# A two-layer hybrid backbone on one core: eight split places, moved modulation, and layer 1's modulation slots as TensorE products

## The chip, the cores and the metric

The kernel runs on one core of a Trainium2 chip. The metric is the device time of one execution in microseconds (us). The profiled execution gives times from its span's start; its granted TensorE clock has two levels, 1.0 (2.4 GHz) and 0.5 (1.2 GHz).

## The reference, cut to what matters

512 latent and 256 context tokens of width 1024 pass through two layers. `w_mod` gives six vectors per layer and per stream, which scale, shift and gate the tokens:

```python
for l in range(DEPTH):
    mod_x = silu(c) @ w_mod[l] + b_mod[l]        # 6 x 1024, latent
    mod_c = silu(c_ctx) @ w_mod[l] + b_mod[l]    # 6 x 1024, context
    mix = token_mixers((h * (1 + ca) + sa) @ w_in[l])     # attention A, B, D and an HGRN2 scan C
    h = layer_norm(ALPHA * h + ga * (mix @ w_out[l]))
    f = conv_ffn(h * (1 + cf) + sf)              # up 1024 -> 2 x 2816, conv of 3, silu(a) * v, down
    h = layer_norm(ALPHA * h + gf * f)
```

The context is dropped after layer 0's last use of it.

## The kernel before, in words

All engines run one hand-ordered program with semaphores. Tokens lie on partitions in `H` (six tiles of 128); a stage first turns them with TensorE transposes (`turn_latent`, `turn_context`), modulates them on the way out of PSUM, and multiplies by weights.

**Weights and ring.** The weights come as 148 slots of 1 MB in the order `STREAM`, loaded by SyncE's queue one after another into a ring of three places, `WR`. `ring_plan` gives each slot a place; a load waits until the slot that held its place is released. SyncE issues in order, so a load also waits for all loads ahead of it. In the FFN only places 1 and 2 are used. A `mod` slot holds 256 columns of `w_mod` (24 slots per layer), an `up` slot the two halves (a and v) of one of 22 FFN column tiles, j = 0 to 21.

**Modulation.** Layer 0's 24 slots are done by TensorE: `mod_products` (8 products in four groups of 32 columns of the array, 16 records), ScalarE copies the rows (`copy_mod`), `mod_columns` adds and turns them (2 products), VectorE adds the bias (`mod_out`). Layer 1's 24 slots lie in layer 0's FFN: VectorE multiplies and adds the slot's eight tiles for both streams (`mod_macs`, 16 operations, releasing the place with `mac_done`), then TensorE sums over partitions (`mod_sums`, 4 products with one column).

**FFN up.** Products are made of two fp32r parts: ScalarE copies the high part of an up half (`high_part`), GpSimd subtracts to the low part (`low_part`, which releases the place with `w_low`), and TensorE does 48 products per half with context (24 of 512 columns, 24 of 256). `first_units` does j = 0, interleaved with the turning of the tokens; `ffn_up` the rest. The high part of half n+2 is made right after half n's sum was read. Two halves are in the split buffer `WS`.

**Out and down projections.** `k_tiles` are 16 (out) or 44 (down) steps. For each, ScalarE writes high parts of the activations and the weight rows into one of `entries` (6 places for out), VectorE (`low_parts`) and GpSimd make the low parts. A place is free when its step is used, or, for the last four steps of each half of the columns, when all tiles of that half are summed (`acc_sum`). VectorE does the first 12 `low_parts` before it takes any sum; then `fold_norm` (three small operations), then per tile: gate, add, statistics; `normalise` follows one tile behind, after GpSimd's power (`rstd_ready`). With context there are 12 sums for 8 PSUM banks, so sum 8 waits until VectorE has read sum 0 (`acc_read`).

**Start.** SyncE loads constants (1.6 MB), x (2.1 MB, issued at 2.1 us), the context (1.05 MB), then slots (1.05 MB each). TensorE waits for both, turns latent (ScalarE copies) and context (VectorE copies), does eight modulation slots, and then the first projection.

Of the kernel before, what the change touches and what calls it, by code (L numbers as in the profile page):

```python
# [7 lines left out]
P = 128  # L8
# [63 lines left out]

def uses():

    u = [("mod", 0, i, 0) for i in range(MOD_FIRST)]
    for l in range(DEPTH):
# [37 lines left out]
def hybrid_backbone(nc, weights, x, ctx_in, consts, masks, params, bias_d, ln_rows, out):  # L114
# [14 lines left out]
    with stack:  # L129
# [20 lines left out]
        EU = nc.alloc_sbuf_tensor_at("EU", [P, 8 * ENTRY], f32r, offset=starts["U"])  # L150
# [3 lines left out]
        def bank(n, cols=512):  # L154
# [6 lines left out]
        entries = ([EU[:, a:a + ENTRY] for a in [e * ENTRY for e in range(5)] + [FT * TOK]],  # L161
                   [t[:, e * ENTRY:(e + 1) * ENTRY] for t in (XH, XL, EW) for e in range(2)])
# [50 lines left out]
        maccs = [W[:, a:a + 1024].rearrange("p (r v c) -> p r v c", r=2, v=2) for a in (5120, 6144)]  # L213
        macc_of = lambda mac: maccs[1][:, mac % 2]
# [63 lines left out]
        xc_raw = sem("xc_raw")  # L278
# [71 lines left out]
        mac_done = sem("mac_done")  # L350
# [234 lines left out]
        def split_parts(q, nt):  # L585

            e = q.entry
            return (e[:, 0:nt * P], e[:, TOK:TOK + nt * P]), (e[:, 2 * TOK:2 * TOK + 512], e[:, 2 * TOK + 512:])
# [34 lines left out]
        def lat_bank(m, k):  # L623
            return bank((4 if m % 2 else 6) + k % 2)

        def ctx_bank(m, k):
            return bank((0, 6, 4)[m] + k % 2, 256)
# [16 lines left out]
        def _(sp):  # L644
# [16 lines left out]
        def _(pe):  # L661
# [20 lines left out]
            def mod_sums(mac, out4):  # L682

                pe.wait_ge(mac_done, mac - (24 - MOD_FIRST))
                for jj in range(2):
                    for v in range(2):
                        mm = pe.matmul(out4[:, 2 * jj + v:2 * jj + v + 1], macc_of(mac)[:, v, jj * P:(jj + 1) * P], ones,
                                       start=True, stop=True)
# [5 lines left out]
            def turn_latent(m, k):  # L694
                freed, count = ((x_raw, 0), (x_val, 0), (x_lat, KT), (x_val, KT))[m]
                if k >= 2:
                    pe.wait_ge(freed, count + k - 1)
                for t in range(NLT):
# [5 lines left out]
            def turn_context(m, k):  # L704
                freed, count = ((xc_raw, 0), (xc_val, 0), (x_ctx, KT))[m]
# [28 lines left out]
            def projections(l, js):  # L734
                for j in js:
# [24 lines left out]
                    mm.then_inc(job_sum, 1)  # L760
                    for n in j.mods:
# [17 lines left out]
            def hgrn(l):  # L779
# [6 lines left out]
                def score_maps(u):  # L786
                    par = u.g % 2
                    pe.wait_ge(qe, u.no + 1)
                    pe.wait_ge(zeroed, l + 2)
# [215 lines left out]
            def ffn_up(l):  # L1005
                us = ups_of[l]
                for u in us[2:]:
                    if u.freed:
                        wait_all(pe, (conv_done, u.freed[0]), (mod_done, u.freed[1]))
                    if u.kind == "mod":  # L1010
                        mod_sums(u.mac, PS[u.pos])
# [9 lines left out]
                    mm.then_inc(up_sum, 1)  # L1021

# [16 lines left out]
        def _(act):  # L1039
# [19 lines left out]
            for k in range(KT):  # L1059
# [5 lines left out]
            def modulate(m):  # L1065
                l, j0, with_ctx = stages[m]
                if m == 0:
                    act.wait_ge(mod_done, MOD_FIRST)
                    act.wait_ge(xc_raw, KT)
                    for k in range(KT):  # L1070
                        c = x3[:, k, SEQ:TOK]
                        act.activation(c, c, ACT.Identity, bias=mod3[:, l, j0 + k, 1:2],
                                       scale=mod3[:, l, j0 + 8 + k, 1:2]).then_inc(x_ctx, 1)
# [131 lines left out]
            def gates(m):  # L1205
# [822 lines left out]
```

## Time and profile before

| | |
|---|---|
| times of three runs | 2188.62, 2193.34, 2197.52 us; median 2193.34 us |
| profiled execution | 2196.59 us, span 2194.1 us, mean granted clock 0.953 |
| busy, share of the span | TensorE 93%, VectorE 60%, GpSimd 39%, ScalarE 34% |
| layer 0's FFN up, j = 1 to 21, at 711.7 to 1108.3 us | 396.6 us |
| layer 0's and layer 1's out projections, from 597.4 and 1740.5 us | 81.0 and 52.2 us |

How to read it: TensorE is busy nearly everywhere, so a change is worth what it takes from or adds to TensorE's own time and its waits. A place where TensorE idles names the engine that ended the wait.

### The profile page before, as it was taken

How to read it: one execution, taken by the hardware profiler on the slowest of the kernel's cores; microseconds unless marked ns; L12 is line 12 of the kernel's file. 1: busy time of each engine (PE TensorE's matmuls, PEld its weight loads, DVE VectorE, ACT ScalarE, POOL GpSimd, SP SyncE). 2: the span in 40 equal slices, each digit the busy share in tenths (PEclk: the TensorE clock that was granted, in tenths of full speed). 3: DMA queues.
4: the chain of work that ended last, by engine and by line, in shares of the span. 5: the costliest groups of instructions: out<-in, count | busy, mean ns of one | idle time of the engine just before them, and what ended most of it. 6: DMA issues, size and time to landing. Idle time of an engine off the chain costs nothing.

```text
span 2194.1 us, 30749 instructions
## 1 busy us (share of the span) xinstructions
PE 2032.8 (93%) x11900; PEld 1640.3 (75%) x11900; DVE 1312.8 (60%) x2695; ACT 744.5 (34%) x1428; POOL 857.2 (39%) x636
## 2 busy tenths in 40 slices
PE   6998999989988799999989999899799978999997
PEld 3665877867767688888878877577787767788786
DVE  2028878776566999889952441775867662222444
ACT  2113343246631222222243321342336623333442
POOL 0005545220134365333443333453511246655643
PEclk8999998999998899999999999998799989999999
DMA  7541010010010323333331111111010112222321
GB/s 299 192 173 39 20 39 20 28 65 1 21 58 20 119 112 134 105 128 115 118 110 54 65 58 58 39 39 39 20 73 2 40 58 77 88 100 99 115 89 68
DMA packets 24127, 169.82 MB, mean 77 GB/s; under 512 B 2608, under 2 KB 2608, under 8 KB 4784
## 3 DMA queue, kind: packets, MB, share of 16 engines
q1 hardware_dynamic: 22544, 157.90, 20.1%
q10 hardware_dynamic: 1440, 9.96, 1.1%
q8 instruction: 96, 1.57, 0.3%
q14 instruction: 47, 0.39, 0.1%
HBM read 165.76 MB, written 2.10 MB: 77 GB/s over the span
## 4 chain that ended last, share of the span: by engine, by line
PE 71%; DVE 14%; issue 6%; POOL 4%; DMA 2%; ACT 2%; SPq 0%; DVEq 0%; ACTq 0%; POOLq 0%
PE PS L1018 20%; PE PS L943 17%; PE PS L758 10%; PE PS L752 7%; DVE W L1334 3%; PE PS L879 3%; PE PS L904 3%; PE PS L863 2%; DMA WR<-in_weights 2%; PE PS L794 2%; PE PS L869 1%; PE PS L999 1%; DVE W L1332 1%; PE PS L671 1%; POOL WS L1901 1%
## 5 line engine op out<-in xcount | busy, mean ns | idle before, releaser
L1018 PE MATMUL PS<-XH,WS 128*128 128x512 f32 x2016 | 545.2, 357 | 8.0 <-POOL WS L1901 7.4
L1018 PEld LDWEIGHTS PS<-XH,WS 128*128 128x128 f32 x2016 | 361.0, 190 | 64.1 <-issue 4.9
L1018 PE MATMUL PS<-XL,WS 128*128 128x512 f32 x1008 | 358.9, 356 | 0.0
L1901 POOL TENSOR_TENSOR WS<-WR,WS 128x1024 fp32r<-128x1024 f32 x88 | 213.1, 2424 | 314.3 <-ACT WS L1203 314.2
L758 PE MATMUL PS<-WR,X 128*128 128x256 f32 x1248 | 292.1, 395 | 5.6 <-DMA WR<-in_weights 5.6
L758 PEld LDWEIGHTS PS<-WR,X 128*128 128x128 f32 x1248 | 246.7, 200 | 43.9 <-DMA WR<-in_weights 6.6
L1258 ACT ACTIVATE W<-PS,PR 128x768 f32<-128x768 f32 (+1 forms) x88 | 77.9, 885 | 450.5 <-PE PS L1018 388.2
L752 PE MATMUL PS<-X,WR 128*128 128x512 f32 (+1 forms) x576 | 210.9, 524 | 10.1 <-issue 6.8
L1018 PEld LDWEIGHTS PS<-XL,WS 128*128 128x128 f32 x1008 | 191.9, 190 | 26.8
L1788 DVE SCALAR_TENSOR_TENSOR W<-PS,PR,W 128x511 f32<-128x511 f32 (+1 forms) x132 | 83.0, 657 | 202.2 <-ACT W L1258 202.1
L1334 DVE SCALAR_TENSOR_TENSOR W<-WR,SC,W 128x256 f32<-128x256 f32 x336 | 199.1, 634 | 6.0
L752 PEld LDWEIGHTS PS<-X,WR 128*128 128x128 f32 x576 | 114.3, 203 | 92.7 <-issue 80.9
L1851 POOL TENSOR_SCALAR W<-U 128x128 f32<-128x128 f32 x48 | 40.5, 844 | 325.2 <-DVE U L1495 201.3
L1890 POOL TENSOR_TENSOR EU<-WR,EU 128x512 fp32r<-128x512 f32 x32 | 52.9, 1681 | 237.6 <-ACT EU L1234 237.5
L943 PE MATMUL PS<-EU 128*128 128x512 f32 x480 | 117.2, 406 | 18.6 <-DVE W L1752 7.9
L943 PE MATMUL PS<-XH 128*128 128x512 f32 x480 | 116.4, 398 | 9.9 <-POOL XH L1890 9.9
L943 PEld LDWEIGHTS PS<-EU 128*128 128x128 f32 x480 | 93.5, 196 | 41.4 <-DVE W L1752 10.5
L943 PEld LDWEIGHTS PS<-XH 128*128 128x128 f32 x480 | 92.3, 193 | 29.9 <-issue 10.4
L1150 ACT ACTIVATE W<-W 128x64 f32<-128x64 f32 (+1 forms) x120 | 35.2, 356 | 203.2 <-DVE W L1524 203.2
L1870 POOL TENSOR_TENSOR W<-W 128x1024 f32<-128x1024 f32 (+1 forms) x48 | 100.0, 2084 | 9.2 <-PE PS L801 9.2
L1593 DVE COPY_PREDICATED W<-MK,PS 128x128 f32<-128x128 uint8 x280 | 93.7, 335 | 14.4 <-PE PS L794 6.7
L1192 ACT ACTIVATE W<-W,ST 128x768 f32<-128x768 f32 (+3 forms) x120 | 95.4, 799 | 12.7 <-DVE ST L1681 9.4
(195 smaller groups left out, 3542.1 us busy)
## 6 DMA issues: line engine op xcount, KB each, us to landing
WR<-in_weights SPq DMA_DIRECT2D x144, 1024.0 KB, 4.8
U<-in_bias ACTq DMA_DIRECT2D x2, 1792.0 KB, 9.6
H<-in_x SPq DMA_DIRECT2D x1, 2048.0 KB, 10.6
U<-in_ln_rows ACTq DMA_DIRECT2D x2, 1024.0 KB, 4.5
W<-in_ln_rows ACTq DMA_DIRECT2D x2, 1024.0 KB, 4.6
WR<-in_weights SPq DMA_DIRECT2D x4, 512.0 KB, 3.4
out_h<-H ACTq DMA_DIRECT2D x4, 512.0 KB, 2.6
H<-in_ctx SPq DMA_DIRECT2D x1, 1024.0 KB, 12.7
```

What stands on the lines that cost most here:

```text
L752: mm = pe.matmul(bank(j.bank)[:, 0:hi - lo], wk[:, k, j.a * P:(j.a + 1) * P], x3[:, k, lo:hi], start=(k == 0), stop=(k == KT - 1))
L758: mm = pe.matmul(bank(j.bank)[:, i * 256:(i + 1) * 256], x3[:, k, t * P:(t + 1) * P], wk[:, k, :], start=(k == 0), stop=(k == KT - 1))
L879: mm = pe.transpose(tb[:, (b - c.lo) * P:(b - c.lo + 1) * P], PB[c.a.r % 2][:, b * P:(b + 1) * P], ident)
L943: mm = pe.matmul(bank((job + 4) % 8), acts[a][:, t * P:(t + 1) * P], rows[b], start=(q.k == 0 and n == 0), stop=(q.k == total - 1 and n == 2))
L1018: mm = pe.matmul(PS[u.pos][:, lo:hi], w[:, part, k, :], src[:, k, lo:hi], start=(k == 0 and src is xh3 and part == 0), stop=(k == KT - 1 a ...
L1192: act.activation(pb, pb, ACT.Exp, bias=s4[:, 3, j:j + 1], scale=-1.0, accum_out=s4[:, 4, j:j + 1]).then_inc(ex, 1)
L1258: act.activation(dst[:, 0:n], PS[u.pos][:, 0:n], ACT.Identity, bias=convp[:, l, 3, jj:jj + 1], scale=convp[:, l, 1, jj:jj + 1]).then_inc(b ...
L1334: ins = dve.scalar_tensor_tensor(acc, wk[:, k, :], scv[:, k, v:v + 1], acc, ALU.mult, ALU.add)
L1593: ins = dve.copy_predicated(dst, msk.broadcast_to([P, 2, 64 // w, w]), src)
L1788: ins = dve.scalar_tensor_tensor(y[:, lo + 1:hi], ps[:, lo:hi - 1], convp[:, l, 0, jj:jj + 1], y[:, lo + 1:hi], ALU.mult, ALU.add)
L1870: pool.tensor_tensor(KE[u.g % 2][:, lo:8, :], EX[u.g % 2][:, 1 + lo:9, :], KB[u.g % 4].unsqueeze(1).broadcast_to([P, 8 - lo, P]), ALU.mult ...
L1901: pool.tensor_tensor(ws5[:, u.c % 2, 1], half_slot(u), ws5[:, u.c % 2, 0], ALU.subtract).then_inc(w_low, 1)
```

## The change

The change, function by function, in the diff below; unchanged lines and repeated patterns are cut.

- `entries[0]` has 8 places; the two new ones are made of two pieces each, so an entry is now a pair.
- Layer 1's 24 modulation slots: `late_products` on TensorE (as `mod_products`, from a zero-padded copy `condf` of the two vectors), ScalarE copies the rows, `late_columns` after the next up half. VectorE's 16 operations and TensorE's four are gone. They stand behind j = 1 to 3 in pairs and behind 4 to 21 singly (before: j = 0, 1 in pairs, 2 to 21 singly).
- The start: TensorE waits for x alone; the context is loaded behind four slots and turned after the first projection; latent copies alternate between ScalarE and VectorE over four banks; VectorE modulates the context from PSUM, and ScalarE's eight operations are gone.
- `normalise` of the first three layer norms goes to ScalarE (two 128x1 operations, one 128x1024), from VectorE (one).
- The scan readout's power on GpSimd is cut into four pieces.

```diff
+def mods_behind(j):
+    return 0 if j == 0 else 2 if j < 4 else 1
...
-            for _ in range(2 if j < 2 else 1):
+            for _ in range(mods_behind(j)):
...
+        whole = lambda e: (e[:, 0:2 * TOK], e[:, 2 * TOK:ENTRY])
+        entries = ([whole(EU[:, a:a + ENTRY]) for a in [e * ENTRY for e in range(5)] + [FT * TOK]]
+                   + [(EV[:, :], EU[:, 12800:13824]), (EU[:, 19456:20992], EU[:, 13824:14848])],
+                   [whole(t[:, e * ENTRY:(e + 1) * ENTRY]) for t in (XH, XL, EW) for e in range(2)])
...
-                release[u.key] = (mac_done, u.mac - (24 - MOD_FIRST))
+                release[u.key] = (mod_prod, u.n + 1)
...
-            sp.dma_start(h3[:, NLT:NT, :], ctx_in.rearrange("(t p) d -> p t d", p=P)).then_inc(h_in, 16)
             for n, key in enumerate(STREAM):
+                if n == 4:
+                    sp.dma_start(h3[:, NLT:NT, :], ctx_in.rearrange("(t p) d -> p t d", p=P)).then_inc(h_in, 16)
...
+            def late_products(u):
+                wk = slot(u.key).rearrange("p (k c) -> p k c", k=KT)
+                pe.wait_ge(condf_ready, 1)
+                for k in range(KT):
+                    rows = slice(32 * (k % 4), 32 * (k % 4) + 32)
+                    mm = pe.matmul(PS[u.pos][rows, 0:256], condf[:, k, :], wk[:, k, :],
+                                   start=(k < 4), stop=(k >= 4), tile_position=(0, 32 * (k % 4)))
+                mm.then_inc(mod_prod, 1)
+
+            def late_columns(u):
+                pe.wait_ge(mod_copied, u.n + 1)
+                for jj in range(2):
+                    mm = pe.matmul(PS[u.pos][:, 256 + 2 * jj:258 + 2 * jj], modrowf[:, u.n % 3, jj * P:(jj + 1) * P], pick,
+                                   start=True, stop=True)
+                mm.then_inc(mod_sum, 1)
...
-            pe.wait_ge(h_in, 32)
+            pe.wait_ge(h_in, 16)
             for k in range(KT):
                 turn_latent(0, k)
-            for k in range(KT):
-                turn_context(0, k)
...
                     mm.then_inc(job_sum, 1)
+                    if opening and l == 0:
+                        for k in range(KT):
+                            turn_context(0, k)
...
                     if u.kind == "mod":
-                        mod_sums(u.mac, PS[u.pos])
+                        late_products(u)
+                        open_mods.append(u)
                         continue
...
                     mm.then_inc(up_sum, 1)
+                    for w in open_mods:
+                        late_columns(w)
+                    open_mods = []
...
+                for t in range(tiles(l)):
+                    b = bnb[:, t, :]
+                    if m < 3:
+                        act.wait_ge(rstd_ready, tiles_before[m] + t + 1)
+                        step(act.activation(b[:, 15:16], b[:, 12:13], ACT.Copy, scale=b[:, 14:15]))
+                        step(act.activation(b[:, 15:16], b[:, 15:16], ACT.Copy, scale=-1.0))
+                        act.activation(h3[:, t, :], h3[:, t, :], ACT.Identity, bias=b[:, 15:16],
+                                       scale=b[:, 14:15]).then_inc(ln_done, 1)
...
-                    if m < 3:
-                        dve.tensor_scalar(h3[:, t, :], h3[:, t, :], b[:, 12:13], b[:, 14:15], ALU.subtract,
-                                          ALU.mult).then_inc(ln_done, 1)
-                        return
...
-                        for q in mods[:2 if u.j < 2 else 1]:
-                            mod_macs(q.key, q.mac)
...
-                pool.tensor_tensor(ross[:, 0:n], ross[:, 0:n], mhalf[:, 0:n], ALU.pow).then_inc(ro_rstd, 1)
+                for c in range(0, n, n // 4):
+                    ins = pool.tensor_tensor(ross[:, c:c + n // 4], ross[:, c:c + n // 4], mhalf[:, 0:n // 4], ALU.pow)
+                ins.then_inc(ro_rstd, 1)
```

**TensorE in layer 0's FFN, between the second half of j = 1 and the first of j = 2.** `XH`, `XL`, `WS` are the up products, `SC` the modulation's. Before:

```order
L1018 MATMUL PS<-XH,WS 128x256
L687 MATMUL PS<-SC,W 128x1 [waits mac_done,mod_done,conv_done]
L687 MATMUL PS<-SC,W 128x1 x3
L687 MATMUL PS<-SC,W 128x1 [waits mac_done,mod_done,conv_done]
L687 MATMUL PS<-SC,W 128x1 x3
L1018 MATMUL PS<-XH,WS 128x512 [waits w_low,mod_done,conv_done]
```

And now:

```order
L1042 MATMUL PS<-XH,WS 128x256
L697 MATMUL PS<-WR,W 32x256 [waits w_arrived2,condf_ready,mod_done,conv_done]
L697 MATMUL PS<-WR,W 32x256 x7
L697 MATMUL PS<-WR,W 32x256 [waits w_arrived1,condf_ready,mod_done,conv_done]
L697 MATMUL PS<-WR,W 32x256 x7
L1042 MATMUL PS<-XH,WS 128x512 [waits w_low,mod_done,conv_done]
```

TensorE now reads the two slots from the ring itself, and the columns (L704, four products) stand behind the next half.

**SyncE's queue around layer 0's first FFN slots.** A row is one load of 1 MB, or several, with what it waits for. Before, the rows are the last `out` slot, up0 and mod0; mod1; up1 and mod2; mod3; up2 and mod4; up3; mod5:

```order
L657 DMA WR<-in_weights 128x2048 [waits rows_low] x3
L657 DMA WR<-in_weights 128x2048 [waits w_low]
L657 DMA WR<-in_weights 128x2048 [waits mac_done] x2
L657 DMA WR<-in_weights 128x2048 [waits w_low]
L657 DMA WR<-in_weights 128x2048 [waits mac_done] x2
L657 DMA WR<-in_weights 128x2048 [waits w_low]
L657 DMA WR<-in_weights 128x2048 [waits mac_done]
```

Now they are the last `out` slot, up0 and up1; mod0 and mod1; up2 and mod2; mod3; up3 and mod4; mod5; up4 and mod6; up5; mod7:

```order
L667 DMA WR<-in_weights 128x2048 [waits rows_low] x3
L667 DMA WR<-in_weights 128x2048 [waits w_low] x2
L667 DMA WR<-in_weights 128x2048 [waits mod_prod] x2
L667 DMA WR<-in_weights 128x2048 [waits w_low]
L667 DMA WR<-in_weights 128x2048 [waits mod_prod] x2
L667 DMA WR<-in_weights 128x2048 [waits w_low]
L667 DMA WR<-in_weights 128x2048 [waits mod_prod] x2
L667 DMA WR<-in_weights 128x2048 [waits w_low]
L667 DMA WR<-in_weights 128x2048 [waits mod_prod]
```

up1 moved ahead of mod0 and mod1. Before, up1's place is freed by mod0's and up2's by mod2's work on VectorE; now up2's place is freed by mod0's products on TensorE, up3's by mod2's and up4's by mod4's. From up5 on an up slot takes the place of the up slot before it (`w_low`), as from up3 on before.

**SyncE at the start.** Before:

```order
L647 DMA H<-in_x 128x4x1024
L648 DMA H<-in_ctx 128x2x1024
L657 DMA WR<-in_weights 128x2048 x3
L657 DMA WR<-in_weights 128x2048 [waits mod_prod] x12
```

And now:

```order
L656 DMA H<-in_x 128x4x1024
L667 DMA WR<-in_weights 128x2048 x3
L667 DMA WR<-in_weights 128x2048 [waits mod_prod]
L659 DMA H<-in_ctx 128x2x1024
L667 DMA WR<-in_weights 128x2048 [waits mod_prod] x11
```

The context's load went behind the fourth slot's, which waits for the first slot's products.

## Rows read from the trace of the kernel before

**Rows 1.** The page, part 4: the chain that ended last, by engine.

```profile
PE 71%; DVE 14%; issue 6%; POOL 4%; DMA 2%; ACT 2%; SPq 0%; DVEq 0%; ACTq 0%; POOLq 0%
```

**Rows 2.** TensorE around both out projections, timeline: start, length, line, count, idle before.

```profile
608.96 26.12 PE L943 MATMUL PS<-EU 128*128 128x512 f32 x114
641.80 1.65 PE L943 MATMUL PS<-EU 128*128 128x512 f32 x3 [6.72 <-DVE W L1752]
...
647.93 30.50 PE L943 MATMUL PS<-EU 128*128 128x512 f32 x129 [0.40 <-DVE W L1752]
...
1740.46 32.89 PE L943 MATMUL PS<-EU 128*128 128x512 f32 x144 [1.97 <-POOL EU L1890]
1779.98 12.68 PE L943 MATMUL PS<-EU 128*128 128x512 f32 x48 [6.63 <-DVE EU L1732]
```

**Rows 3.** ScalarE and VectorE beside them, timelines.

```profile
633.76 0.85 ACT L1233 ACTIVATE EU<-X 128x768 fp32r<-128x768 f32 x1 [14.95 <-PE PS L943]
...
611.86 9.55 DVE L1732 TENSOR_TENSOR EU<-X,EU 128x768 fp32r<-128x768 f32 x5 [0.30 <-ACT EU L1233]
...
634.64 0.96 DVE L1732 TENSOR_TENSOR EU<-X,EU 128x768 fp32r<-128x768 f32 x1 [13.23 <-ACT EU L1233]
```

**Rows 4.** Windows after a wait: us, busy of TensorE (count), granted clock, DMA, GB/s.

```profile
642.00:650.00 8.00, 6.81 (x14) 0.50 0.11 45
```

**Rows 5.** Windows of layer 0's FFN up: busy of PE, PEld, DVE, ACT, POOL, clock, DMA.

```profile
862.90:1109.50 246.60, 246.60 (x1461) 219.47 (x1461) 217.33 (x357) 62.33 (x69) 90.98 (x41) 1.00 0.35 124
```

**Rows 6.** The first waited slot of the FFN, timelines of VectorE, ScalarE, GpSimd.

```profile
708.01 6.38 DVE L1334 SCALAR_TENSOR_TENSOR W<-WR,SC,W 128x256 f32<-128x256 f32 x14
...
719.27 1.06 ACT L1203 ACTIVATE WS<-WR 128x1024 fp32r<-128x1024 f32 x1 [7.57 <-DMA WR<-in_weights]
...
720.40 4.83 POOL L1901 TENSOR_TENSOR WS<-WR,WS 128x1024 fp32r<-128x1024 f32 x2 [13.13 <-ACT WS L1203]
```

**Rows 7.** TensorE's price of one modulation slot, and what starts behind it, timeline.

```profile
62.00 0.50 PE L678 MATMUL PS<-SC,W 128*128 128x2 f32 x4
...
62.43 2.10 PE L671 MATMUL PS<-WR,W 128*32 128x256 f32 x32
...
72.31 1.07 PE L671 MATMUL PS<-WR,W 128*32 128x256 f32 x16
...
73.31 3.72 PE L752 MATMUL PS<-X,WR 128*128 128x256 f32 x16
...
967.52 0.95 PE L687 MATMUL PS<-SC,W 128*128 128x1 f32 x8
...
968.33 0.47 PE L1018 MATMUL PS<-XH,WS 128*128 128x512 f32 x1
```

**Rows 8.** The start: TensorE's timeline, x's load (us to landing), a window.

```profile
15.37 6.19 PE L701 MATMUL PS<-CN,H 128*128 128x128 f32 x32 [15.37 <-DMA H<-in_ctx]
...
24.98 1.93 PE L671 MATMUL PS<-WR,W 128*32 128x256 f32 x32
...
43.35 1.93 PE L671 MATMUL PS<-WR,W 128*32 128x256 f32 x16
...
H<-in_x SPq DMA_DIRECT2D x1, 2048.0 KB, 10.6
...
28.00:32.00 4.00, 2.03 (x33) 0.98 (x21) 0.16 (x1) 0.38 (x1) 0.00 (x0) 1.00 0.98 410
```

**Rows 9.** The readout's power in both layers, and VectorE's wait for it, timelines.

```profile
469.21 4.16 POOL L1877 TENSOR_TENSOR ST<-ST,SC 128x24 f32<-128x24 f32 x1
...
473.41 0.96 DVE L1623 TENSOR_TENSOR U<-U,ST 128x768 f32<-128x768 f32 x1 [2.06 <-POOL ST L1877]
...
1642.79 2.90 POOL L1877 TENSOR_TENSOR ST<-ST,SC 128x16 f32<-128x16 f32 x1
```

**Rows 10.** VectorE's normalise at layer 0's first norm, timeline.

```profile
679.71 0.80 DVE L1718 TENSOR_SCALAR H<-H,ST 128x1024 f32<-128x1024 f32 x1
...
682.91 0.81 DVE L1718 TENSOR_SCALAR H<-H,ST 128x1024 f32<-128x1024 f32 x1
```

More of the change, by code:

```diff
@@ L277, in hybrid_backbone @@
         x_raw = sem("x_raw")
-        xc_raw = sem("xc_raw")
+        xd_raw = sem("xd_raw")
         x_val = sem("x_val")
@@ L623, in lat_bank @@
         def lat_bank(m, k):
-            return bank((4 if m % 2 else 6) + k % 2)
+            return bank((0, 1, 6, 7)[k % 4] if m == 0 else (4 if m % 2 else 6) + k % 2)
         def ctx_bank(m, k):
-            return bank((0, 6, 4)[m] + k % 2, 256)
+            return bank((6, 6, 4)[m] + k % 2, 256)
         restored = [tiles(0), NLT, NLT]
@@ L704, in turn_context @@
             def turn_context(m, k):
-                freed, count = ((xc_raw, 0), (xc_val, 0), (x_ctx, KT))[m]
+                freed, count = ((x_ctx, 0), (xc_val, 0), (x_ctx, KT))[m]
+                if m == 0 and k == 0:
+                    pe.wait_ge(h_in, 32)
                 if k >= 2:
@@ L1021, in ffn_up @@
                     mm.then_inc(up_sum, 1)
+                    for w in open_mods:
+                        late_columns(w)
+                    open_mods = []
+                for w in open_mods:
+                    late_columns(w)
             for l in range(DEPTH):
@@ L1057, in copy_mod @@
                 act.activation(modrow[:, n % 4, :], mod_bank(n)[:, 0:256], ACT.Copy).then_inc(mod_copied, 1)
-            for k in range(KT):
+            for k in range(0, KT, 2):
                 act.wait_ge(tp_lat, k + 1)
@@ L1067, in modulate @@
                 if m == 0:
[L1068 to L1073, printed above, removed]
+                    return
                 elif m == 2:
@@ L1250, in ffn @@
                 real = [u for u in ups_of[l] if u.kind == "up"]
-                for n_u, u in enumerate(real):
+                n_u = -1
+                for u in ups_of[l]:
+                    if u.kind == "mod":
+                        act.wait_ge(mod_prod, u.n + 1)
+                        if u.n >= 27:
+                            act.wait_ge(mod_sum, u.n - 2)
+                        act.activation(modrowf[:, u.n % 3, :], PS[u.pos][:, 0:256], ACT.Copy).then_inc(mod_copied, 1)
+                        continue
+                    n_u += 1
                     jg = FT * l + u.j
@@ L1351, in mod_out @@
                     dve.tensor_tensor(o, s3, b, ALU.add).then_inc(mod_done, 1)
-            for k in range(KT):
-                dve.wait_ge(tp_ctx, k + 1)
-                dve.tensor_copy(x3[:, k, SEQ:TOK], ctx_bank(0, k)).then_inc(xc_raw, 1)
+            for k in range(1, KT, 2):
+                dve.wait_ge(tp_lat, k + 1)
+                dve.tensor_copy(x3[:, k, 0:SEQ], lat_bank(0, k)).then_inc(xd_raw, 1)
             for i in range(MOD_FIRST):
@@ L1762, in residual @@
                             dve.tensor_scalar(b[:, 14:15], b[:, 13:14], EPS, None, ALU.add).then_inc(bn_ready, 1)
-                            if t >= 1:
+                            if m == 3 and t >= 1:
                                 normalise(t - 1)
-                normalise(nt - 1)
+                if m == 3:
+                    normalise(nt - 1)
             def ffn(l):
@@ L1771, in ffn @@
                     dve.wait_ge(xc_low, KT)
-                mods = [u for u in ups_of[l] if u.kind == "mod"]
+                if has_ctx(l):
+                    dve.memset(condf.rearrange("p k c -> p (k c)"), 0.0).then_inc(zeroed, 1)
+                    dve.wait_ge(zeroed, 3)
+                    dve.tensor_copy(condf[:, :, 0:2], scv).then_inc(condf_ready, 1)
                 for u in ups_of[l]:
-                    if u.kind == "up" and u.half == 0:
-                        for q in mods[:2 if u.j < 2 else 1]:
-                            mod_macs(q.key, q.mac)
-                        mods = mods[2 if u.j < 2 else 1:]
                     if u.kind == "mod":
-                        dve.wait_ge(mod_sum, MOD_FIRST + u.mac)
-                        mod_out(u.l + 1, u.j, PS[u.pos][:, 0:4])
+                        dve.wait_ge(mod_sum, u.n + 1)
+                        mod_out(u.l + 1, u.j, PS[u.pos][:, 256:260])
                         continue
```

58 lines of the change are left out of this document (19 added, 39 removed).

## The prediction, written before the result

> **What bounds the kernel now.** I read the chain of waits first: TensorE holds 71% of it [rows 1]. So I then followed TensorE's timeline for its waits, and at each wait the timeline of the engine that ended it. The reader should see in [rows 2] that both out projections stop in the middle for 6.6 to 6.7 us until VectorE has done something, in [rows 5] that the FFN's main part has no wait at all (TensorE busy 246.6 of 246.6 us), and in [rows 6] that the FFN's beginning waits for slots. Whatever the change adds to TensorE in a full stretch costs its whole length; whatever it removes from VectorE there is worth nothing.
>
> **Eight split places, layer 0's out projection.** With six places, ScalarE can't fill the place of step 10 until the first half of the columns is summed (idle 14.95 us, to 633.76 [rows 3]). VectorE does step 10's and 11's low parts (from 634.64 [rows 3]) and the fold before it takes the first sum, and TensorE needs that sum's bank: 6.72 us of waiting, to 641.80, then products at the lower clock (0.50 over 642 to 650 [rows 4]). With eight places, steps 8 to 11 take the places of steps 0 to 3, used long before. The low parts go on at 9.55/5 = 1.91 us each from 611.86 [rows 3]: eight of them (4 to 11) end at about 626, the fold at about 628, before TensorE starts the second half at about 634. Steps 12 to 15 then need filling before the eight steps' midpoint, 72 products later. The second half's 144 products take 32.89 us when nothing stops them (as many do in layer 1 [rows 2]). It begins about 1.4 us before the first row's end at 608.96 + 26.12 = 635.1, since six of its products lie in that row; so it ends at 633.7 + 32.9 = 666.6 instead of 647.93 + 30.50 = 678.4: **-11.9 us**.
>
> **Layer 1's.** The wait before 1779.98 goes (6.63 us), and the 48 products behind it take 48 x 32.89/144 = 11.0 us instead of 12.68 [rows 2]: **-8.3 us**. Together -20.2. The bounds are -24 (small waits elsewhere go as well) and -14 (the waits alone, and some of them left: low parts are slow while GpSimd works beside VectorE).
>
> The Trainium skill, SBUF — State Buffer, on contention, says that a VectorE operation with two SBUF inputs and a GpSimd operation lock each other out of a shared port pair for whole instructions; the low parts are such operations, and this trace agrees: 1.91 us with GpSimd at work beside them, 0.96 us for the one at 634.64. By that rule 12 low parts in a row would keep VectorE slow; even then they end before 634, so the sum is the same.
>
> **The FFN of layer 0.** Each modulation slot now costs TensorE its products, 73.31 - 72.31 = 1.00 us at the full clock, and its columns, 62.43 - 62.00 = 0.43 us; what goes is 968.33 - 967.52 = 0.81 us [rows 7]. That is +0.62 us per slot, and there is no wait for it to fall into from j = 5 on. The 16 VectorE operations per slot are off the path there. A column tile without its slot takes 246.6/14 - 0.81 = 16.80 us [rows 5].
>
> The first tiles decide the rest. up1's load is no longer behind mod0, so after ScalarE's read of the first half (ended 719.27 - 7.57 = 711.7) only its high and low part are left, 1.06 + 2.42 us: up1 starts at 715.3, a wait of 3.6 us. But up2 waits for mod0's products, which stand behind all of j = 1. From the release of a place to a usable low part the trace shows 708.01 + 6.38 = 714.4 to 720.40 + 2.42 = 722.8, 8.4 us [rows 6]; mod1's products fill 1.0 of it. So TensorE waits 7.4 us before j = 2, and in the same way before j = 3 (behind mod2) and j = 4 (behind mod4). Before each, the first products run at the lower clock again: in [rows 2] 48 products after such a wait took 1.7 us more; four waits, 6.8 us.
>
> Sum, from 711.7: 3.6 + 21 x 16.80 + 23 x 1.43 (the last slot falls into the wait before the down projection) + 3 x 7.4 + 6.8 = 3.6 + 352.8 + 32.9 + 22.2 + 6.8 = 418.3 us. It was 396.6, so **+21.7 us**. Bounds: +28 if each wait also delays the slots' loads by a slot's length; +14 if the waits come to what they were (then 24 x 0.62 = 14.9 is left).
>
> The Trainium skill, TensorEngine Tiling (Array Packing), Key Properties, says that changing the tiling mode drains TensorE, which speaks against 24 such slots between full-array products; its table promises up to 4x for 32 columns. The 1.00 us holds both switches, since it runs from the slot's first product to the next full one. By the 4x alone, 16 passes at the 0.22 us of a 256-column pass would be 0.89 us, and the sum 2.6 us less; the row decides.
>
> **The start.** TensorE waits for x alone, which lands at 2.1 + 10.6 = 12.7 instead of the 15.37 at which both were in. The latent turn had one copying engine and two banks and took 6.2 us; with two and four it is some 2 us shorter, and the context turn (24.98 - 21.56 = 3.4 us) moves behind the first projection. But the eighth slot can't be in before all bytes ahead of it: 1.6 + 2.1 + 1.05 + 8 x 1.05 = 13.2 MB, at 410 GB/s [rows 8] from 2.3 us on some 35, with landing and the queue's gaps 37.4 instead of the 43.35 at which its products began. So -6.0 us there; the context turn with VectorE's modulation in it costs 3.4 to 5.5 us on TensorE, I take 4.5. **-1.5 us**, bounds -6 (the turn falls into waits for slots that come later) and +1.
>
> **The power.** 24 columns take 4.16 us and 16 take 2.90 [rows 9], so 0.157 us per column and 0.38 us per instruction. Three more instructions: +1.15 us, and VectorE waits for it already in layer 0 (2.06 us). In layer 1 the same. **+2.3 us**, bounds 0 (the fixed part overlaps) and 2.5.
>
> **Normalise.** At layer 0's first norm VectorE needs 682.91 - 679.71 = 3.20 us per tile [rows 10], TensorE delivers one per 12 x 0.228 = 2.74 us (a product's time from layer 1's row in [rows 2]). Without its normalise VectorE keeps up, and hands over about 1 us earlier; with the first two latent tiles modulated in the meantime I take -1.8. At the second norm TensorE is the slower one, ScalarE's three operations replace one on the last tile and stand ahead of its own modulation: +0.7. Third: 0. **-1.1 us**, bounds -3 and +3.
>
> **Sum.** -20.2 + 21.7 - 1.5 + 2.3 - 1.1 = +1.2 us. The profiled execution, 2196.6 us, becomes 2197.8; it lies 3.3 us above the median of the three runs, 2193.34, so that median becomes **2194.5 us**.
>
> **Rivals.** All against 2193.34; 0.5%, 11 us, is about what a measurement of this kernel can tell from no change.
> - *The slots are nearly free on TensorE.* If products and columns cost no more than the 0.81 us they replace, because four column groups overlap with the neighbours, the FFN is at +6.8 and the whole at 2180: faster. Against it stands the 1.00 us in [rows 7], taken between full products. It decides from 1.0 us per slot instead of 1.43. With the start at its better bound it needs less. Chance 0.14.
> - *The places don't help.* If VectorE's first sum in layer 0 comes after 636, since 12 low parts beside GpSimd get slower than 1.91 us, TensorE waits as before: 8 to 12 us are not gained, and the whole is at 2206: slower. The point is 2.9 us per low part. Chance 0.06.
> - *Up slots late at every tile.* From j = 5 on an up slot's load is issued about 4.5 us after the tile before (read 1, high part 1.06, low part 2.42), takes 719.27 - 714.4 = 4.9 [rows 6], and the low part must be there 18 us after it; were a modulation slot's load ahead of it for 8 us more, each of 17 tiles would wait 1 us or more: 2212, slower. The slack speaks against it. Chance 0.08.
> - *The waits before j = 2, 3 and 4 are hidden*, as nothing was changed there: 2180 to 2186. Only if the loads were issued earlier than the queue's order allows; chance 0.04, on both sides of the bound.
> - My forecast, 0.68.
>
> **How the numbers follow.** The range 2182 to 2207 takes in the bounds of the FFN, and of the places down to the second rival's edge; the forecast's own is 2186 to 2203. Faster by over 0.5% 0.16, within 0.71, slower 0.13.
>
> **What would show it.** Right: no wait of TensorE over 1 us inside either out projection, VectorE's first sum before 634 in layer 0; in the FFN three waits of 7 to 8 us before j = 2, 3, 4, then a period of 18.2 us instead of 17.6; the eighth slot's products at about 37; the power at 5.3 and 4.1 us. Wrong: a period of 17.6 (products free), or out projections still longer than 70 and 45 us.

## The result, and the profile after

| | before | changed |
|---|---|---|
| median of 12 runs, us | 2191.29 | 2199.59 (2198.4 to 2202.1) |
| ratio, 95% interval | | 1.0033, 1.0023 to 1.0044: 5 to 10 us slower |
| profiled execution's span, us | 2194.1 | 2199.9 |
| VectorE busy, share of the span | 60% | 48% |

The forecast of 2194.5 us was 5 us short: the time lies in its range, 2182 to 2207, and within 0.5% of before. The ratios leave out two executions at a far lower clock, one of the kernel before (3315.7 us, mean granted clock 0.567) and one of the late pairs below (2608.9 us, 0.737).

In the chain of work that ended last, by engine, VectorE's 14% [rows 1] became 8%, and TensorE's share rose:

```profile
PE 77%; DVE 8%; issue 5%; POOL 5%; DMA 2%; ACT 2%; DVEq 0%; SPq 0%; ACTq 0%; POOLq 0%
```

I cut both traces at the same TensorE products (us from the span's start):

| stage | before | changed | difference | forecast |
|---|---|---|---|---|
| span's start to layer 0's out projection | 597.4 | 593.2 | -4.2 | -0.3 |
| from there to the end of FFN tile j = 0 | 114.3 | 98.6 | -15.8 | -13.7 |
| FFN of layer 0, j = 1 to 21 | 396.6 | 422.3 | +25.7 | +21.7 |
| from there to layer 1's out projection | 632.2 | 635.9 | +3.7 | +1.9 |
| from there to layer 1's down projection | 319.8 | 314.5 | -5.3 | -8.3 |
| down projection to the end | 133.9 | 135.5 | +1.6 | 0 |
| sum | 2194.1 | 2199.9 | +5.8 | +1.2 |

(The forecast column splits the power between the first and fourth row and the norms between the second and fourth, and is rounded.)

TensorE's timeline in the out projections of the changed kernel (layer 0, then layer 1), beside [rows 2]:

```profile
603.19 9.80 PE L965 MATMUL PS<-EU 128*128 128x512 f32 x42
...
627.11 18.52 PE L965 MATMUL PS<-EU 128*128 128x512 f32 x81
...
659.75 0.84 PE L965 MATMUL PS<-EU 128*128 128x512 f32 x3
...
1749.98 12.53 PE L965 MATMUL PS<-EU 128*128 128x512 f32 x54 [1.62 <-POOL EU L1910]
...
1785.53 0.97 PE L965 MATMUL PS<-EU,EV 128*128 128x512 f32 x3 [1.26 <-DVE EV L1750]
```

Neither wait of 6.6 us is left; layer 1 keeps 1.26 us. VectorE's timeline of layer 0 shows why: the fold (L1420) and the first sum (L1770) stand ahead of 627, where the second half of the columns runs without a stop.

```profile
619.50 1.26 DVE L1420 TENSOR_TENSOR ST<-MOD,PR 128x16 f32<-128x16 f32 x1
...
621.09 0.68 DVE L1770 TENSOR_TENSOR W<-PS,W 128x512 f32<-128x512 f32 x1
```

The beginning of the FFN on TensorE: the slots' products (L697), and the wait before j = 2; the same before j = 3 and 4; then the windows around the first of them (busy of PE, PEld, DVE, ACT, POOL, granted clock, DMA share, GB/s):

```profile
695.16 0.80 PE L1042 MATMUL PS<-XH,WS 128*128 128x512 f32 x1 [3.41 <-POOL WS L1921]
...
713.55 1.93 PE L697 MATMUL PS<-WR,W 128*32 128x256 f32 x32
723.03 0.77 PE L1042 MATMUL PS<-XH,WS 128*128 128x512 f32 x1 [7.55 <-POOL WS L1921]
...
753.19 0.76 PE L1042 MATMUL PS<-XH,WS 128*128 128x512 f32 x1 [7.58 <-POOL WS L1921]
```

```profile
715.00:720.00 5.00, 0.48 (x12) 0.00 (x0) 0.00 (x0) 0.60 (x1) 0.00 (x0) 0.89 0.83 316
720.00:725.00 5.00, 1.97 (x5) 1.61 (x6) 2.28 (x4) 4.95 (x7) 4.47 (x2) 0.50 0.25 103
725.00:730.00 5.00, 5.00 (x15) 3.89 (x14) 0.00 (x0) 0.00 (x0) 4.92 (x4) 0.58 0.60 210
```

During the wait the DMA brings up2, and mod2 behind it (316 GB/s). The clock then is 0.50 to 0.58 for 10 us. The waits of the stage, before and then changed (us in total, times, longest):

```profile
PE PS L687 <- DVE W L1334: 18.1, 7, 9.6
```

```profile
PE PS L1042 <- POOL WS L1921: 26.3, 4, 7.7
```

And one tile of the full part:

```profile
875.62 1.07 PE L697 MATMUL PS<-WR,W 128*32 128x256 f32 x16
876.62 0.50 PE L1042 MATMUL PS<-XH,WS 128*128 128x512 f32 x1
...
884.94 0.28 PE L1042 MATMUL PS<-XH,WS 128*128 128x256 f32 x1
885.07 0.50 PE L704 MATMUL PS<-SC,W 128*128 128x2 f32 x4
885.43 0.47 PE L1042 MATMUL PS<-XH,WS 128*128 128x512 f32 x1
...
893.96 1.07 PE L697 MATMUL PS<-WR,W 128*32 128x256 f32 x16
```

The period is 893.96 - 875.62 = 18.34 us. Before, it was 246.6/14 = 17.61 [rows 5], 16.80 without the slot. So a slot costs TensorE 1.54 us, not 1.43: the columns stand between the halves now, and ahead of the products the gap is 0.21 us where it is 0.13 between halves.

### The profile page after: what moved, and what is told of

The parts are those of the page before. It is cut to its first block, busy times and chain, and to the rows that moved or that the text cites. A ratio compares the mean times of both kernels' runs of the same rounds, so it can differ in the third digit from the quotient of the medians.

```text
span 2199.9 us, 31017 instructions
## 1 busy us (share of the span) xinstructions
PE 2044.3 (93%) x12188; PEld 1639.8 (75%) x12188; DVE 1048.0 (48%) x2301; ACT 771.3 (35%) x1488; POOL 852.5 (39%) x642
## 4 chain that ended last, share of the span: by engine, by line
PE 77%; DVE 8%; issue 5%; POOL 5%; DMA 2%; ACT 2%; DVEq 0%; SPq 0%; ACTq 0%; POOLq 0%
PE PS L1042 25%; PE PS L965 17%; PE PS L777 10%; PE PS L771 7%; PE PS L901 3%; PE PS L926 3%; PE PS L885 2%; DMA WR<-in_weights 2%; PE PS L816 2%; PE PS L1021 1%; POOL WS L1921 1%; PE PS L891 1%; PE PS L697 1%; PE PS L681 1%; DVE EU L1750 1%
## 5 line engine op out<-in xcount | busy, mean ns | idle before, releaser
L1042 PE MATMUL PS<-XH,WS 128*128 128x512 f32 x2016 | 555.0, 361 | 33.6 <-POOL WS L1921 33.6
L771 PE MATMUL PS<-X,WR 128*128 128x512 f32 (+1 forms) x576 | 208.8, 520 | 10.4 <-issue 6.6
L1227 ACT ACTIVATE WS<-WR 128x1024 fp32r<-128x1024 f32 x88 | 92.1, 1049 | 43.9 <-DMA WR<-in_weights 41.6
L965 PE MATMUL PS<-EU 128*128 128x512 f32 x420 | 99.4, 390 | 3.7 <-POOL EU L1910 3.7
L1216 ACT ACTIVATE W<-W,ST 128x768 f32<-128x768 f32 (+3 forms) x120 | 95.4, 799 | 13.5 <-DVE ST L1703 10.4
L965 PE MATMUL PS<-XL 128*128 128x512 f32 x420 | 98.9, 389 | 0.0
```

Of the source, the lines that this page charges most:

```text
L771: mm = pe.matmul(bank(j.bank)[:, 0:hi - lo], wk[:, k, j.a * P:(j.a + 1) * P], x3[:, k, lo:hi], start=(k == 0), stop=(k == KT - 1))
L965: mm = pe.matmul(bank((job + 4) % 8), acts[a][:, t * P:(t + 1) * P], rows[b], start=(q.k == 0 and n == 0), stop=(q.k == total - 1 and n == 2))
L1042: mm = pe.matmul(PS[u.pos][:, lo:hi], w[:, part, k, :], src[:, k, lo:hi], start=(k == 0 and src is xh3 and part == 0), stop=(k == KT - 1 a ...
L1216: act.activation(pb, pb, ACT.Exp, bias=s4[:, 3, j:j + 1], scale=-1.0, accum_out=s4[:, 4, j:j + 1]).then_inc(ex, 1)
L1227: act.activation(ws5[:, u.c % 2, 0], half_slot(u), ACT.Copy).then_inc(w_high, 1)
```

## The experiments

All are given as the ratio to the kernel before, run beside them (medians 2190.6 to 2193.6 us); "against the changed kernel" is the difference of two ratios times 2191, with both intervals combined 3 to 6 us either way.

| run | median, us | ratio, 95% interval | against the changed kernel |
|---|---|---|---|
| six places | 2219.6 | 1.0128 (1.0111 to 1.0144) | +21 |
| old FFN | 2172.6 | 0.9918 (0.9902 to 0.9934) | -25 |
| before, with eight places | 2175.0 | 0.9922 (0.9905 to 0.9939) | |
| one power | 2194.9 | 1.0014 (1.0004 to 1.0024) | -4 |
| late pairs | 2188.6 | 0.9982 (0.9967 to 0.9996) | -11 |
| half steps | 2169.3 | 0.9892 (0.9869 to 0.9915) | -31 |
| one column group | 2250.6 | 1.0262 (1.0235 to 1.0289) | +50 |
| slots on VectorE, late pairs | 2167.2 | 0.9883 (0.9862 to 0.9905) | -33 |
| half steps and more | 2164.7 | 0.9872 (0.9854 to 0.9891) | -35 |
| half steps on VectorE | 2197.8 | 1.0012 (0.9997 to 1.0027) | -5 |
| normalise on VectorE | 2195.3 | 1.0015 (1.0004 to 1.0025) | -4 |
| old start | 2201.2 | 1.0040 (1.0025 to 1.0055) | +2 |

**Theory**: the split places gain their 20 us, and the FFN gives back more, by slots that cost TensorE its time and by an order of slots that makes up2 to up4 late. **Rivals**: the gain is only displaced; the FFN is longer because it begins earlier; the waits belong to its beginning and not to the pairs.

### Six places in the changed kernel

```diff
-                   + [(EV[:, :], EU[:, 12800:13824]), (EU[:, 19456:20992], EU[:, 13824:14848])],
+                   ,
```

> The changed kernel with six split places for the out projections instead of eight; all else as changed. Theory (the places are worth what the two stages lost in the profiles, 81.1 - 67.4 = 13.7 us in layer 0 and 52.2 - 45.4 = 6.8 us in layer 1): 2199.6 + 20.5 = 2220 us, and TensorE waits again for 6 to 7 us in the middle of both stages. Rival (part of the 13.7 us in layer 0 is only an earlier, better fed beginning of the stage, and layer 1's is as small for another reason): 2212 us or less.

Measured: +20.0 us by the medians, so the rival falls. TensorE's wait is there again, in layer 0 to the hundredth, and in layer 1 longer than before the change (7.82 instead of 6.63 us). Layer 0, then layer 1:

```profile
633.65 1.65 PE L965 MATMUL PS<-EU 128*128 128x512 f32 x3 [6.72 <-DVE W L1770]
...
1801.17 9.14 PE L965 MATMUL PS<-EU 128*128 128x512 f32 x32 [7.82 <-DVE EU L1750]
```

A small part of the rival is true all the same. In layer 0 the stage takes 80.4 us here, 81.1 before the change and 67.4 in the changed kernel, and its first 36 products 8.40, 10.05 and 8.45 us: of the 13.7 us between the two profiles, 1.6 come from a quicker beginning and not from the places.

### The old FFN in the changed kernel

```diff
-                        late_products(u)
-                        open_mods.append(u)
+                        mod_sums(u.mac, PS[u.pos])
...
+                        for q in mods[:mods_behind(u.j)]:
+                            mod_macs(q.key, q.mac)
```

> The changed kernel with layer 1's modulation slots back on VectorE, in the old order (in pairs behind j = 0 and 1); places, start, normalise and power as changed. Theory (the FFN stage's whole +26.8 us is the slots' work on TensorE and the order that came with it): 2199.6 - 26.8 = 2173 us, the period per column tile 17.6 us. Rival (part of the +26.8 us comes because the stage now begins 21 us earlier, before its slots are in): 2180 us or more.

Measured 2172.6 us. The rival falls: in the new surroundings the old FFN waits as it did before (18.6 us for VectorE's L1352, longest 9.6), and the stage takes 397.1 us.

### Eight places alone, before the other changes

```diff
-        entries = ([EU[:, a:a + ENTRY] for a in [e * ENTRY for e in range(5)] + [FT * TOK]],
+        entries = ([whole(EU[:, a:a + ENTRY]) for a in [e * ENTRY for e in range(5)] + [FT * TOK]]
+                   + [(EV[:, :], EU[:, 12800:13824]), (EU[:, 19456:20992], EU[:, 13824:14848])],
```

> The kernel before with eight split places and nothing else. Theory: 2191.3 - 20.5 = 2171 us, no wait of TensorE over 1.5 us inside either out projection. Rival (VectorE, which here still normalises, falls behind at the first norm and gives 2 to 4 us back): 2175 us.

Measured 2175.0 us (2167.9 to 2180.6), 17 us less (13 to 21). The median is the rival's, but the interval holds the theory's 2171 us as well: this does not tell them apart. Its trace is the useful part. From the out projection to the end of tile j = 0 it takes 98.6 us, as the changed kernel does, though VectorE still normalises. (The trace is of the fastest of the six executions, 2167.9 us.)

### One power

```diff
-                for c in range(0, n, n // 4):
-                    ins = pool.tensor_tensor(ross[:, c:c + n // 4], ross[:, c:c + n // 4], mhalf[:, 0:n // 4], ALU.pow)
-                ins.then_inc(ro_rstd, 1)
+                pool.tensor_tensor(ross[:, 0:n], ross[:, 0:n], mhalf[:, 0:n], ALU.pow).then_inc(ro_rstd, 1)
```

> The changed kernel with the scan readout's power as one instruction again. Theory (each layer loses about 1 us to the wait and as much again because TensorE runs longer at the lower clock behind it; the profiles show +2.2 and +2.4 us): 2199.6 - 4.6 = 2195 us. Rival (only the three instructions' fixed part, 1.04 us per layer): 2197.5 us.

Measured 4.7 us less by the medians (1 to 7 with both intervals). The four pieces take 5.20 us (x4) in layer 0 and 3.93 us in layer 1, as forecast (4.16 and 2.90 in [rows 9]). In layer 1 TensorE's wait is 4.14 us instead of 3.11, and behind it the clock is 0.66, where the single power leaves it at 1.00. First a window of the changed kernel from the end of its wait, then one of this run, which holds the wait (to 1659.1) and what follows:

```profile
1663.00:1668.00 5.00, 4.41 (x34) 3.12 (x36) 4.31 (x15) 2.00 (x6) 1.10 (x1) 0.66 0.01 3
```

```profile
1655.00:1665.00 10.00, 6.89 (x71) 5.29 (x73) 9.93 (x20) 4.39 (x11) 4.61 (x1) 1.00 0.01 2
```

The traces bear this out better than the interval does. From TensorE's short wait for ScalarE ahead of the readout (0.79 us, at 1634.04 in the changed kernel) to layer 1's out projection, all eight traces with four pieces take 115.94 to 115.96 us, and the four of the changed kernel's variants with one power 113.56 to 113.58: 2.4 us, of which 1.03 is the wait. In layer 0 the same stretch takes 146.5 to 147.3 and 145.0 to 145.1 us. So 4.5 us stand in every one of these traces, and the rival falls.

### The pairs late

```diff
-    return 0 if j == 0 else 2 if j < 4 else 1
+    return 0 if j == 0 else 2 if j > 18 else 1
```

> The changed kernel with the three pairs of modulation slots behind j = 19, 20 and 21 instead of 1, 2 and 3. Theory (a pair behind a tile makes the next up slot's load wait for the pair's first products, wherever it stands): no wait before j = 3 and 4 but 7.6 us before j = 20 and 21; the third pair ends with the FFN, where the down projection's first steps wait anyway: 2199.6 - 7.6 - 2 (lower clock behind the wait) = 2190 us. Rival (the waits belong to the stage's beginning, where the slots have not been loaded yet): all three go, 2172 us.

Measured 2188.6 us (forecast 2190). The waits moved with the pairs, to before j = 20 and 21 (7.8 and 7.6 us), and the early ones are gone, so the rival's 2172 us falls. The order makes them, not the stage's beginning.

### The pairs taken apart (half steps)

```diff
+MOD_TIMES = [(j, e) for j in range(1, FT) for e in ((0.5, 0.95) if 2 <= j < 5 else (0.95,))]
...
+            loads = [(j - 0.8, ("up", l, j, 0)) for j in range(FT)]
+            loads += [(ends[n - 1][0] if n else 0.5, key) for n, (_, key) in enumerate(ends)]
```

> The changed kernel with the pairs of modulation slots taken apart: of the slots used around j = 2, 3 and 4 one stands between the two halves of the tile and one behind it, and the up slot's load is issued ahead of the one behind the tile. TensorE does the same products. Theory: the three waits of 7.55 to 7.6 us and the lower clock behind them go, the stage takes 4.4 + 21 x 16.88 + 24 x 1.46 + 2 = 396 instead of 423.4 us: 2172 us. Rival (half a tile, 8.4 us, is too short for issue, load and landing, so that TensorE waits for each slot in the middle of a tile instead): 2185 us or more.

Measured 2169.3 us, 30 us less than the changed kernel (25 to 36). TensorE's waits in the stage are 3.4 us before j = 1 and 1.1 us behind the last slot; the slots in the middle arrive in time.

### All eight products in one column group

```diff
-                    rows = slice(32 * (k % 4), 32 * (k % 4) + 32)
-                    mm = pe.matmul(PS[u.pos][rows, 0:256], condf[:, k, :], wk[:, k, :],
-                                   start=(k < 4), stop=(k >= 4), tile_position=(0, 32 * (k % 4)))
+                    mm = pe.matmul(PS[u.pos][0:32, 0:256], condf[:, k, :], wk[:, k, :],
+                                   start=(k == 0), stop=(k == KT - 1), tile_position=(0, 0))
```

> The changed kernel with all eight products of each of layer 1's modulation slots in one group of 32 columns of the array instead of four; the other three groups' partial sums are left out, so layer 1's modulation has stale values in them. Theory (the groups overlap, and 16 passes one after another take 16 x 0.12 = 1.9 us instead of 1.09): 24 x 0.85 = +20 us, 2220 us. Rival (the 1.09 us are mostly the change of the tiling around the products, and the groups bring nothing): 2200 to 2204 us.

Measured 51 us more. The direction is the theory's, the size missed both expectations: I took half of a pass's time. The trace has 878.25 - 874.68 = 3.57 us from a slot's first product to the next full one, 0.223 per record, as any 256-column record in one place:

```profile
874.68 3.64 PE L696 MATMUL PS<-WR,W 128*32 128x256 f32 x16
878.25 0.50 PE L1041 MATMUL PS<-XH,WS 128*128 128x512 f32 x1
```

So four groups do in 1.00 us what one does in 3.57. The Trainium skill, TensorEngine Tiling (Array Packing), Theoretical Speedup, gives up to 4x for a dimension of 32 and under; here it is 3.6x, with the switches to and from this mode in both times. Of the 24 slots 23 lie in the stage (the last falls into the wait before the down projection), and 23 times 2.57 is 59 us; 8 of them come back since the four waits sum to 18.3 instead of 26.3 us, the longer products standing where TensorE would wait. That leaves 51 us, and the stage is 473.2 - 422.3 = 50.9 us longer.

### Slots on VectorE, pairs late, one power, second norm on VectorE

```diff
-    return 0 if j == 0 else 2 if j < 4 else 1
+    return 0 if j == 0 else 2 if j > 18 else 1
...
-                    if m < 3:
+                    if m in (0, 2):
                         act.wait_ge(rstd_ready, tiles_before[m] + t + 1)
```

with the two edits of the old FFN and of the power.

> Eight places and the new start, the slots on VectorE but in the new order with the pairs behind j = 19, 20 and 21, the readout's power as one instruction, the second norm's normalise back on VectorE. Theory: from the version with the old FFN, 2172.6, less 16.1 - 4.4 = 11.7 us (the first pair of slots no longer stands before j = 1), 2 us of lower clock behind it, 4.7 us of power and 1.5 us of the second norm: 2153 us. Rival (the late pairs, 14.6 us of VectorE beside 4.5 us of its other work in a tile of 17.6 us, hold TensorE's banks up at three tiles): 2160 us or more.

Measured 2167.2 us: in the rival's range, 14 us over the theory. up1 starts after 3.41 us of waiting, as meant, but the first late pair comes 5.89 us late:

```profile
1046.95 1.84 PE L697 MATMUL PS<-SC,W 128*128 128x1 f32 x8 [5.89 <-DVE W L1352]
```

With six shorter ones the waits for slots sum to 11.9 us. The stage takes 394.2 us, 2.9 less than the old FFN's 397.1, where the theory had 11.7 + 2 less. Of the missing 10.8 us the late pair is 5.89; the rest is not settled.

### Half steps with one power and the second norm on VectorE

The edits are those of the half steps, the power and the norm together.

> The version with the pairs taken apart (slots on TensorE, no waits before j = 2 to 4), and on top the power as one instruction and the second norm's normalise back on VectorE. Theory: 2169.3 - 4.7 - 1.5 = 2163 us. Rival (the power's lower clock behind the wait was a matter of chance, so that only the wait's 1 us per layer comes back): 2166 us.

Measured 2164.7 us (2164.5 to 2166.1), 1.3% faster than before (1.1 to 1.5%), the best of all, though its interval overlaps those of the half steps alone and of the slots on VectorE with late pairs. By its time it lies between the two expectations. Its trace speaks against the rival: behind the readout's wait in layer 1 it has the 113.56 us of every single power.

### Half steps on VectorE

```diff
+                    if u.kind == "up" and mods:
+                        n = 24 - len(mods)
+                        if MOD_TIMES[n] == ((u.j, 0.95) if u.half == 0 else (u.j + 1, 0.5)):
+                            q = mods.pop(0)
+                            mod_macs(q.key, q.mac)
```

> As the version before it (pairs taken apart, one power, second normalise on VectorE), but the slots on VectorE, and the three additional slots in the middle of j = 6, 11 and 16, each computed on VectorE a tile earlier, behind the conv of a first half. Theory: TensorE pays 0.81 us per slot instead of 1.56, 24 x 0.75 = 18 us less, and waits 2 to 4 us where VectorE and GpSimd work side by side: 2163 - 18 + 3 = 2148 us. Rival (VectorE's slots take up to 12.6 us beside GpSimd, so they come late at the first tiles and at the three additional slots): 2158 us or more.

A miss by 50 us: 2197.8 us, as slow as the changed kernel; what the rival feared (2158 us or more) came, and more of it. TensorE waits 29.5 us for slots, in eight waits, and 3.4 us for bank space. In the middle of j = 6 and behind it, TensorE and then VectorE:

```profile
806.70 1.84 PE L712 MATMUL PS<-SC,W 128*128 128x1 f32 x8 [7.99 <-DVE W L1367]
...
825.78 1.84 PE L712 MATMUL PS<-SC,W 128*128 128x1 f32 x8 [6.79 <-DVE W L1367]
```

```profile
812.95 0.61 DVE L1365 TENSOR_SCALAR W<-WR,SC 128x256 f32<-128x256 f32 x2 [3.89 <-DMA WR<-in_weights]
813.60 12.03 DVE L1367 SCALAR_TENSOR_TENSOR W<-WR,SC,W 128x256 f32<-128x256 f32 x14
```

VectorE's 14 operations take 12.03 us where they took 6.38 [rows 6], while GpSimd makes two low parts and a product of the gated halves beside them (6.9 us in all); and since the slot in the middle is freed late, the next one's load is late as well (3.89 us).

### Normalise on VectorE in the changed kernel

```diff
-                    if m < 3:
+                    if m < 0:
                         act.wait_ge(rstd_ready, tiles_before[m] + t + 1)
```

and the `tensor_scalar` back in VectorE's `normalise`.

> The changed kernel with normalise on VectorE in all norms, as before. Theory, by the handovers in the two profiles: +2.3 us at layer 0's first norm, -1.7 us at the second, +0.7 us at the third: 2199.6 + 1.3 = 2201 us. Rival (without its normalise VectorE gains nothing at the first norm in the new surroundings; the 2.3 us are GpSimd's and the clock's): 2197 to 2198 us.

Measured 4.3 us less than the changed kernel by the medians (1 to 7 with both intervals): neither expectation. The handover at the first norm is as I read it: 8.95 us from the out projection's end to tile j = 0 on ScalarE's version, 11.3 us here. But tile j = 0 then takes 22.2 us there and 19.9 us here. Windows of the changed kernel, then of this run:

```profile
665.00:667.00 2.00, 1.28 (x6) 1.28 (x7) 0.54 (x1) 1.71 (x3) 0.74 (x1) 0.50 0.00 0
...
671.00:673.00 2.00, 2.00 (x8) 1.71 (x7) 0.00 (x0) 0.00 (x0) 2.00 (x3) 0.50 0.00 0
```

```profile
665.00:667.00 2.00, 0.95 (x3) 0.55 (x4) 1.84 (x3) 0.28 (x1) 0.12 (x1) 0.50 0.00 0
...
671.00:673.00 2.00, 2.00 (x13) 1.73 (x12) 0.31 (x1) 0.83 (x2) 2.00 (x3) 1.00 0.00 0
```

In the changed kernel the low clock lasts into the dense products, to 674; here it falls into the waits and is over soon after 669. In ten more traces with ScalarE's normalise that tile takes 21.6 to 22.4 us, in the two with VectorE's and eight places 19.9 us each. Before the change, with VectorE's and six places, it took 22.0 as well, so who normalises does not decide it alone. The first norm's gain is nothing: the two stages together take 98.6 us either way. At the second norm ScalarE costs 11.28 against 10.18 us from the first turn to the first projection; in all traces it is 10.8 to 12.1 us with ScalarE's and 10.2 to 10.4 with VectorE's.

Much of the rest lies where the two kernels are the same. Layer 0's down projection begins behind a wait of 3.66 and 3.65 us; its first 36 products then take 11.31 us in the changed kernel (granted clock 0.66 over 1120 to 1130) and 8.45 in this run (1.00):

```profile
1122.35 11.31 PE L965 MATMUL PS<-XH 128*128 128x512 f32 x36 [3.66 <-POOL XH L1910]
```

```profile
1121.60 8.45 PE L965 MATMUL PS<-XH 128*128 128x512 f32 x36 [3.65 <-POOL XH L1913]
```

Behind layer 1's out projection TensorE needs 391.9 us to its last product in the changed kernel and 389.1 here, but 388.9 in the run with the old start, where ScalarE normalises. So of the 4 us about 1 is shown to be the norm's own, at the second norm; the rest comes with the clock behind waits, and that it would come back in each execution is not shown.

### The old start in the changed kernel

```diff
-                if n == 4:
-                    sp.dma_start(h3[:, NLT:NT, :], ctx_in.rearrange("(t p) d -> p t d", p=P)).then_inc(h_in, 16)
...
-            pe.wait_ge(h_in, 16)
+            pe.wait_ge(h_in, 32)
             for k in range(KT):
                 turn_latent(0, k)
+            for k in range(KT):
+                turn_context(0, k)
```

> The changed kernel with the old start: context loaded ahead of the slots and turned before the first slot, one copying engine for the latent turn, the context modulated by ScalarE. Theory (the -1.5 us of the forecast, which the profile shows at 56 us): 2199.6 + 1.5 = 2201 us. Rival (the further 5 us that the profile of the changed kernel is ahead between 109 and 148 us belong to the start too): 2206 us.

Measured +1.6 us by the medians, and not distinguishable from none (-2 to +6): the rival's 6.4 us is just outside. The 5 us that the profile of before loses from 109 us on are its own: 32 products take 10.22 us there behind a wait of 3.07, and 7.17 us behind 3.08 in the run with eight places alone, whose start is the same. The 16 products behind the next wait (2.20 and 2.19 us), with the gap to the next slot's columns, take 5.24 and 3.56 us: together 4.7 us.

```profile
114.69 10.22 PE L758 MATMUL PS<-WR,X 128*128 128x256 f32 x32 [3.07 <-DMA WR<-in_weights]
```

```profile
114.48 7.17 PE L761 MATMUL PS<-WR,X 128*128 128x256 f32 x32 [3.08 <-DMA WR<-in_weights]
```

## Why the prediction was nearly right, step by step

- **Split places, -20.2**: right, mechanism and size. Undone, +20.0 us; alone, -17 (13 to 21). In the profiles layer 0 gave more than forecast (67.4 instead of 81.1 us for the stage), but 1.6 us of that is the quicker beginning; layer 1 gave less (45.4 instead of 52.2), since the low parts of step 14, 2.87 us beside GpSimd, left 1.26 us of waiting. The first sum is at 621, well ahead of the 634 forecast as needed. The rival that the places don't help fell.
- **FFN, +21.7**: the mechanism was right and the size short: +25.7 in the trace, 25 to 27 us in the run with the old FFN. The waits were right: 3.41 (3.6), and 7.55, 7.58 and 7.7 us (7.4). The term "23 x 1.43" measured 1.54: +2.5 us. Another 0.5 us is the waits, and what is left for the lower clock is 7.8 instead of 6.8. The rival "nearly free" fell, that of late up slots at every tile too: from j = 5 on there is no wait.
- **Start, -1.5**: the sum was right, -1.4 us at 56 us in the traces (undone, 1.6 us, within the noise), but by luck: two terms missed by about 1.4 us each, in opposite directions. The eighth slot's products came at 38.81 instead of the 37.4 forecast, and the moved context turn cost 3.1 us instead of 4.5. Nor did the bytes set the eighth slot's time: TensorE waits for the fifth slot, and the next three follow at the lower clock, 2.81 us each, without a wait. The same three steps lie between 34.92 and 43.35 before the change.

```profile
30.39 1.93 PE L681 MATMUL PS<-WR,W 128*32 128x256 f32 x16 [4.93 <-DMA WR<-in_weights]
...
38.81 1.93 PE L681 MATMUL PS<-WR,W 128*32 128x256 f32 x16
```

- **Power, +2.3**: the durations were right, the term was short and its upper bound of 2.5 too low. "Three more instructions" left out what the longer wait does to the clock behind it: 4.5 us in the traces, 4.7 by the medians.
- **Normalise, -1.1**: this step failed. "Hands over about 1 us earlier" was true, by 2.3 us, and worth nothing; the step took the products behind the handover as unchanged in length. At the second norm it had +0.7, measured about 1.1. So the term was about +1 instead of -1.1; that undoing it gave some 4 us is more than the norm's own stretches show.
- Against before the change it is +7 us by the ratio where the sum said +1.2, so 6 us are missing. The FFN holds 4 of them, the power and the normalise a good 2 each; that is 2 too much, with every difference of runs uncertain by some 3 us. The traces alone show +5.8 us, less than the ratio, since the profile of before has the chance loss of 5 us at its start. That the absolute forecast came within 5 us has a little luck in it: it was counted from the median of three runs, 2193.34 us, 2 us above that of twelve.

## What to carry to other kernels

When work moves onto the engine that is the bound, the price is its whole length there (1.54 us instead of 0.81, 24 times), and an order of loads that suited the old owner of the work must be made anew: here the order alone was worth 30 us, more than the price (24 times 0.73 is 18). Ask of each buffer's next load who frees the place, and when, in units of the bound's own steps; two slots behind one tile made TensorE wait 7.6 us for the next tile's weights, one in the middle and one behind it did not. And a handover that comes earlier is worth only what is still ahead after the products behind it have been timed at the clock that they then get.

## What the hardware showed beyond that

- Four groups of 32 columns do 16 records of 256 columns in 1.00 us; one group takes 3.57 us.
- The same products behind the same wait ran at the lower clock in one execution and not in another: 32 of them took 10.22 us behind 3.07 us and 7.17 behind 3.08 at the start, 36 took 11.31 us behind 3.66 and 8.45 behind 3.65 at the down projection. That is 3 us each time, the first in a profile that a forecast was read from.
- Dense work that began 1.2 us later had the full clock from its first product, and took 19.9 instead of 22.2 us. Counted from the beginning of the out projection both end at 98.6 us.
- 14 VectorE operations of 256 columns took 6.38 us alone, and 12.03 us beside 6.9 us of GpSimd's work.
